# Projection start of a hybrid decoder block: fillers, first tile, first slab and first query slab cut differently

## The reference, cut to what matters

```
h = rmsnorm(x) * norm_mix
proj = h @ w_in      # q_sb,k_sb,v_sb | q_sa,k_sa,v_sa | q_idx,k_idx,w_idx | g_sb,g_sa
o_sb = stick_breaking(rmsnorm(q_sb), rmsnorm(k_sb), v_sb)
o_sa = topk_attention(rmsnorm(q_sa), rmsnorm(k_sa), v_sa, q_idx, k_idx, w_idx)
x = x + (sigmoid(g_sb) * (o_sb @ w_sb) + sigmoid(g_sa) * (o_sa @ w_sa)) @ w_out
x = x + relu(rmsnorm(x) @ w_ff1)^2 @ w_ff2
```

## Time and profile before

| | |
|---|---|
| median of 3 runs | 735.97 us (735.78 to 736.24) |
| the profiled execution | 735.93 us, of which the span is 734.2 us |
| PE busy | 727.6 us (99%) |
| DVE, ACT, POOL busy | 521.4, 336.4, 228.6 us |
| DMA moved | 70.64 MB |

### The profile page before, as it was taken

The page is one execution under the profiler, slowest core; times in us unless marked ns, Lnnn a source line. Parts: engine busy times, 40 slices in busy tenths (PEclk is TensorE's granted clock), DMA queues, the critical chain, the costliest instruction groups (busy, mean ns, idle before and its releaser), DMA issues.

```text
span 734.2 us, 9810 instructions
## 1 busy us (share of the span) xinstructions
PE 727.6 (99%) x3508; PEld 581.9 (79%) x3508; DVE 521.4 (71%) x737; ACT 336.4 (46%) x481; POOL 228.6 (31%) x194
## 2 busy tenths in 40 slices
PE   8999999999999999999999999999999999999998
PEld 5878878787777666788888988888888888888887
DVE  6355886899996755647556569695968779595972
ACT  6244753454666777723324353524335252534320
POOL 4105326000002555003301082624427080815610
PEclk9999999999999999999999999999999999999999
DMA  9308231310111212133090135142330505131102
GB/s 323 145 15 256 88 116 58 115 58 21 39 58 57 58 58 58 58 114 115 12 339 24 57 115 172 58 151 78 111 117 23 206 0 171 57 114 57 58 15 101
DMA packets 44038, 70.64 MB, mean 96 GB/s; under 512 B 2657, under 2 KB 27489, under 8 KB 44002
## 3 DMA queue, kind: packets, MB, share of 16 engines
q1 hardware_dynamic: 44000, 70.16, 29.2%
q10 hardware_dynamic: 2, 0.00, 0.0%
HBM read 65.71 MB, written 2.10 MB: 92 GB/s over the span
## 4 chain that ended last, share of the span: by engine, by line
PE 95%; DVE 1%; ACT 1%; POOL 1%; issue 1%; DMA 0%; ACTq 0%; DVEq 0%
PE ps L1754 7%; PE ps L1756 7%; PE ps L1755 7%; PE ps L419 7%; PE ps L421 7%; PE ps L420 7%; PE ps L412 7%; PE ps L414 6%; PE ps L1782 6%; PE ps L413 6%; PE ps L1784 6%; PE ps L1783 6%; PE ps L1592 2%; PE ps L1636 2%; PE ps L1668 1%; PE ps L1678 1%
## 5 line engine op out<-in xcount | busy, mean ns | idle before, releaser
L1754 PE MATMUL ps<-b_hi,cut_hi 128*128 128x512 f32 (+1 forms) x280 | 104.0, 371 | 0.0
L1755 PE MATMUL ps<-b_lo,cut_hi 128*128 128x512 f32 (+1 forms) x280 | 103.8, 371 | 0.0
L1756 PE MATMUL ps<-b_hi,cut_lo 128*128 128x512 f32 (+1 forms) x280 | 103.8, 371 | 0.0
L419 PE MATMUL ps<-cut_hi,a_hi 128*128 128x512 f32 x224 | 90.3, 403 | 0.7 <-DVE cut_lo L403 0.7
L421 PE MATMUL ps<-cut_hi,a_lo 128*128 128x512 f32 x224 | 87.6, 391 | 0.0
L420 PE MATMUL ps<-cut_lo,a_hi 128*128 128x512 f32 x224 | 87.6, 391 | 0.0
L403 DVE TENSOR_TENSOR cut_lo<-raw,cut_hi 128x2048 fp32r<-128x2048 f32 (+2 forms) x36 | 59.9, 1664 | 31.4 <-ACT cut_hi L395 31.4
L888 ACT ACTIVATE qo_sb<-ps 128x512 f32<-128x512 f32 x32 | 19.2, 600 | 135.6 <-PE ps L1756 90.9
L623 POOL TENSOR_TENSOR a_lo<-qo_sb,a_hi 128x512 fp32r<-128x512 f32 x49 | 78.2, 1619 | 5.6 <-ACT a_hi L898 5.6
L611 POOL TENSOR_SCALAR qo_sb<-qo_sb 128x128 f32<-128x128 f32 (+3 forms) x28 | 33.3, 1189 | 118.9 <-DVE snmax L1193 117.9
L395 ACT ACTIVATE cut_hi<-raw 128x2048 fp32r<-128x2048 f32 (+2 forms) x33 | 49.3, 1495 | 32.8 <-PE ps L414 22.7
(11 more groups left out here) (193 smaller groups left out, 1652.3 us busy)
## 6 DMA issues: line engine op xcount, KB each, us to landing
raw<-in_w_ff_dram SPq DMA_DIRECT2D x32, 1024.0 KB, 5.6
raw<-in_w_in_dram SPq DMA_DIRECT2D x16, 1024.0 KB, 5.6
gates<-in_x_dram SPq DMA_DIRECT2D x8, 512.0 KB, 5.9
raw<-in_w_out_dram SPq DMA_DIRECT2D x4, 1024.0 KB, 5.1
raw<-in_w_in_dram SPq DMA_DIRECT2D x4, 512.0 KB, 7.4
raw<-in_w_branch_sb_dram SPq DMA_DIRECT2D x2, 1024.0 KB, 5.0
raw<-in_w_branch_sa_dram SPq DMA_DIRECT2D x4, 512.0 KB, 6.0
out_dram<-gates SPq DMA_DIRECT2D x7, 256.0 KB, 2.0
```

The costliest lines, as they stand in the source:

```text
L419: nc.tensor.matmul(dst, l_hi, w_hi, start=start, stop=False)
L1754: T.matmul(dst, w_hi[:, w], b_hi[:, k, a:b], start=(k == 0), stop=False)
L1755: T.matmul(dst, w_hi[:, w], b_lo[:, k, a:b], start=False, stop=False)
L1756: mm = T.matmul(dst, w_lo[:, w], b_hi[:, k, a:b], start=False, stop=(k == KD - 1))
```

## The change

- The fillers' data (`cold_b`, zeros) is made first thing on DVE, without waiting for POOL, and a semaphore `cold_made` tells PE. The fillers use it as weights too. There are now six of them ahead of the gain row's spread, five behind it and seven after the first tile's transposes (before: none, four and three).
- Tile 0 is scaled in two halves of 512 columns, and each group of transposes waits for its own half.
- The first half of slab 0 is loaded, rounded and subtracted as two blocks (quarters of the slab), and the second of them is loaded behind tile 1 of x. Its rounding stands behind tile 0's first turned half on ACT.
- On DVE tile 1 is scaled ahead of the low part of tile 0's second turned half.
- Slab 2 (the first query slab) is rounded and subtracted in two halves, and PE waits for the second only at its third block.

```diff
-WARM = (4, 3)
+WARM = (6, 5, 7)
...
-            load_half(0, 0)
+            def load_quarter(k):
+                sp.dma_start(raw[:, 0, k * 512:(k + 1) * 512], rows(win, P * k, 1, GROUPS[KVI], 512).rearrange("p k c -> p (k c)")
+                             ).then_inc(half_in[k], 16)
+
+            load_quarter(0)
             sp.dma_start(x_tok[:, 1, :], x_d[P:2 * P, :]).then_inc(x_in[1], 16)
+            load_quarter(1)
             load_half(0, 1)
             load_half(1, 0)
             load_half(1, 1)
...
-                    pool.wait_ge(half_hi, 2)
-                    pool.wait_ge(half_cut, 1)
+                    pool.wait_ge(half_hi, 3)
+                    pool.wait_ge(half_cut, 2)
...
+            def act_quarter(k):
+                act.wait_ge(half_in[k], 16)
+                A(cut_slot(0, cut_hi, k, 4), raw[:, 0, k * 512:(k + 1) * 512], ACT.Copy).then_inc(half_hi, 1)
...
                 if m == 0:
-                    act_half(0)
+                    act_quarter(0)
                 elif m == 1:
                     norm_hi(0, a_hi)
+                    act_quarter(1)
                     act.wait_ge(raw_in[0], 16)
                     act_cut(0, 1, 2)
                     norm_hi(1, a_hi)
...
-                if g != KSB:
+                if g == KVI:
+                    act_half(2)
+                    act_cut(2, 1, 2)
+                elif g != KSB:
                     act_cut(2 * g + 2)
...
+            link(V.memset(cold_b[:, :], 0.0))
+            V.tensor_copy(kw_gap, cold_b[:, 0:24 * KD].rearrange("p (k c) -> p k c", k=KD)).then_inc(cold_made, 1)
             dve.wait_ge(ident_done, 1)
             dve.wait_ge(const_made, 1)
-            link(V.memset(cold_b[:, :], 0.0))
-            V.tensor_copy(kw_gap, cold_b[:, 0:24 * KD].rearrange("p (k c) -> p k c", k=KD))
...
-            norm_scale(0, x_tok[:, 0, :], x_tok[:, 0, :], mix_gain)
-            dve_half(0)
+            for hf in range(2):
+                norm_scale(0, x_tok[:, 0, hf * S:(hf + 1) * S], x_tok[:, 0, hf * S:(hf + 1) * S], bank(6 + hf))
+            dve_quarter(0)
             norm_lo(0, a_hi, a_lo)
+            dve_quarter(1)
             dve_cut(0, 1, 2)
+            norm_scale(1, x_tok[:, 1, :], x_tok[:, 1, :], mix_gain)
             norm_lo(1, a_hi, a_lo)
-            norm_scale(1, x_tok[:, 1, :], x_tok[:, 1, :], mix_gain)
             dve_cut(1, 1, 2)
...
-                if g != KSB:
+                if g == KVI:
+                    dve.wait_ge(half_hi, 4)
+                    V.tensor_tensor(cut_slot(2, cut_lo, 0, 2), raw[:, 2, 0:SLAB // 2],
+                                    cut_slot(2, cut_hi, 0, 2).bitcast(F32), ALU.subtract).then_inc(half_cut, 1)
+                    dve_cut(2, 1, 2)
...
-                pe.wait_ge(row_scaled, m + 1)
                 for hf in range(2):
                     u = 2 * m + hf
+                    pe.wait_ge(row_scaled, 1 + hf if m == 0 else m + 2)
...
-                    T.matmul(bank(3), ident_b, cold_b[:, :], start=True, stop=True)
-
+                    T.matmul(bank(3), cold_b[:, 0:P], cold_b[:, :], start=True, stop=True)
+
+            pe.wait_ge(cold_made, 1)
+            keep_warm(WARM[0])
             pe.wait_ge(one_row_made, 1)
...
-            pe.wait_ge(const_cut, 1)
-            keep_warm(WARM[0])
+            keep_warm(WARM[1])
...
-                        pe.wait_ge(half_cut, half + 1)
+                        pe.wait_ge(half_cut, 3 if half else 1)
                         pe.wait_ge(nt_cut, half + 1)
+                    if first and k == 1 and not half:
+                        pe.wait_ge(half_cut, 2)
...
+                    if (g, half, m, k) == (QSB, 0, 0, 2):
+                        slab_ready(SL_PROJ + 2 * QSB)
...
-                slab_ready(SL_PROJ + 2 * g + half)
+                if (g, half) == (QSB, 0):
+                    pe.wait_ge(half_cut, 4)
+                else:
+                    slab_ready(SL_PROJ + 2 * g + half)
...
-            keep_warm(WARM[1])
+            keep_warm(WARM[2])
```

More of the change, by code:

```diff
@@ L229, in block_kernel @@
         gains_in = sem("gains_in")
-        half_in = [sem(f"half_in{j}") for j in range(2)]
+        half_in = [sem(f"half_in{j}") for j in range(3)]
         half_hi = sem("half_hi")
@@ L264, in block_kernel @@
         kix_low = sem("kix_low")
+        cold_made = sem("cold_made")
         kix_out = sem("kix_out")
@@ L442, in load @@
                 if i == RAW + 1:
-                    sp.wait_ge(half_cut, 2)
+                    sp.wait_ge(half_cut, 3)
                 for p0, np_, nk, src in slab_source(i):
@@ L451, in load_half @@
                 sp.dma_start(dst[:, 2 * hf:2 * hf + 2, :], rows(win, 512 * i + 256 * hf, 2, GROUPS[KVI], 512)
-                             ).then_inc(raw_in[i] if hf else half_in[i], 16)
-            load_half(0, 0)
+                             ).then_inc(raw_in[i] if hf else half_in[2], 16)
+            def load_quarter(k):
+                sp.dma_start(raw[:, 0, k * 512:(k + 1) * 512], rows(win, P * k, 1, GROUPS[KVI], 512).rearrange("p k c -> p (k c)")
+                             ).then_inc(half_in[k], 16)
+            load_quarter(0)
             sp.dma_start(x_tok[:, 1, :], x_d[P:2 * P, :]).then_inc(x_in[1], 16)
+            load_quarter(1)
             load_half(0, 1)
@@ L662, in norm_hi @@
                   bank(4 + u % 2).rearrange("p (a b) -> p a b", a=4), ACT.Copy).then_inc(nt_hi, 1)
+            def act_quarter(k):
+                act.wait_ge(half_in[k], 16)
+                A(cut_slot(0, cut_hi, k, 4), raw[:, 0, k * 512:(k + 1) * 512], ACT.Copy).then_inc(half_hi, 1)
             def act_half(i):
-                act.wait_ge(half_in[i], 16)
-                A(cut_slot(i, cut_hi, 0, 2), raw[:, i, 0:SLAB // 2], ACT.Copy).then_inc(half_hi, 1)
+                if i == 1:
+                    act.wait_ge(half_in[2], 16)
+                else:
+                    act.wait_ge(*slab_arrived(i))
+                    act.wait_ge(*slab_used(i - CUT))
+                A(cut_slot(i, cut_hi, 0, 2), raw[:, i % RAW, 0:SLAB // 2], ACT.Copy).then_inc(half_hi, 1)
             act.dma_start(mix_row, norm_mix).then_inc(mix_row_in, 16)
@@ L1020, in norm_lo, with dve_quarter @@
                                 ALU.subtract).then_inc(nt_cut, 1)
[L1022 to L1025, removed]
+            def dve_quarter(k):
+                dve.wait_ge(half_hi, k + 1)
+                V.tensor_tensor(cut_slot(0, cut_lo, k, 4), raw[:, 0, k * 512:(k + 1) * 512],
+                                cut_slot(0, cut_hi, k, 4).bitcast(F32), ALU.subtract).then_inc(half_cut, 1)
             mix_gain = ps[:, 6 * S:8 * S]
             dve.wait_ge(mix_spread, 1)
-            norm_scale(0, x_tok[:, 0, :], x_tok[:, 0, :], mix_gain)
-            dve_half(0)
+            for hf in range(2):
+                norm_scale(0, x_tok[:, 0, hf * S:(hf + 1) * S], x_tok[:, 0, hf * S:(hf + 1) * S], bank(6 + hf))
+            dve_quarter(0)
             norm_lo(0, a_hi, a_lo)
+            dve_quarter(1)
             dve_cut(0, 1, 2)
+            norm_scale(1, x_tok[:, 1, :], x_tok[:, 1, :], mix_gain)
             norm_lo(1, a_hi, a_lo)
-            norm_scale(1, x_tok[:, 1, :], x_tok[:, 1, :], mix_gain)
             dve_cut(1, 1, 2)
```

## The result

The changed kernel takes 737.40 us (median of 14 runs, 735.14 to 737.90) against 735.79 us for the kernel before (14 runs, 735.64 to 736.24): ratio 1.0018, 95% interval 1.0011 to 1.0025. It is slower by 1.6 us. I had forecast 734.7 us, 1.3 us faster. Twelve of the changed kernel's runs lie between 737.17 and 737.90, two at 735.14 and 735.19; the kernel before has no such gap.

What follows compares the result with a forecast made beforehand. PE, busy 99% of the span, was taken as the bound. Span 734.2 - 0.3 (start) - 0.96 (slab 2 halves) = 732.9, plus 1.7 us around it, gave 734.7 us, range 734.1 to 736.2.

Steps and rivals of the forecast that it cites:

- I take a rise near 4.8, just behind the six fillers.: At the start, PE's clock goes from 1.2 to 2.4 GHz near 4.8 us, so the spread ends at 6.2.
- 1.9 us behind the start of full-array work: Clock timing read from the earlier trace: second run of full-array work began at 9.66, the clock rose at 11.6.
- the 7.0 of the other count: Clock rise if counted from the first full-array work (6.14 to 11.6): at 7.0 us, with 0.5 us less won.
- Rival 1: At the start, clock stays at 1.2 GHz until 11.6: 2.0 us lost, 0.96 won, 737.0 us; chance 0.12.
- Tile 1 then lands at about 7.05: Start loads: with a quarter slab less in front, tile 1 of x lands at 7.05 instead of 7.87.
- The forecast gain of 0.3 us at the start: Tile 0's second projection half: PE's second matmul at 14.62 against 14.92; gain 0.3 us, between 0 and 0.65.
- rival 3: Tile 1 lands no sooner; the quarter lengthens ACT's queue by 0.48 us: 0.3 lost, 0.96 won, 735.3; chance 0.10.
- Halves of slab 2: gain 0.96 us.: Query projection near 40 us: slab 2 in halves removes PE's wait, 0.96 us gained and passed to the end.
- Slab 0's second half lands at 9.23 again.: Start loads: the same bytes lie ahead of this half as before, so its landing stays at 9.23.
- DVE and GpSimd: Shared port at the start: DVE's subtract of slab 0 (done 11.6) must precede POOL's at 11.83, or 0.3 us goes.
- The wait for tile 3's scaling: PE's 0.4 us wait in a chain starting at its own transposes; forecast to move along with them.
- The range: Whole-kernel time meant to hold 8 in 10: 734.1 to 736.2 us, from rival 2 to above rival 4.

Runs made afterwards that it cites:

- experiment 5: Changed kernel with fourteen fillers ahead of the gain row's spread, none between spread and transposes, seven behind; 737.10 us (735.80 to 738.35), before 736.01.
- experiment 3: Changed kernel with six fillers ahead of the spread, but four and three behind it as before; 736.95 us, before 735.96.
- experiment 6: Kernel before with only the early fillers' data and six fillers ahead of the spread added, four and three behind; 737.50 us, before 736.01.
- experiment 10: Changed kernel with slab 0's first half in one piece as before, all fillers kept (six, five, seven); 737.82 us, before 735.99.
- experiment 2: Changed kernel without fillers ahead of the spread, four and three behind as before; 735.27 us, before 735.96.
- experiment 1: Kernel before with only query slab 2 rounded and subtracted in two halves; 734.71 us, before 735.96, ratio 0.9983.
- experiment 8: Changed kernel with the gain row's spread made by matmuls over all 128 array rows instead of one; 738.60 us, before 736.01.
- experiment 7: Changed kernel with two, four and three fillers and slab 0's first half in one piece as before; 735.09 us, before 736.01.
- experiment 9: Kernel before with slab 2 in halves and tile 0 scaled in two halves, fillers and loads as before; 735.29 us, before 735.99.

## Why the prediction was wrong, step by step

- **"I take a rise near 4.8, just behind the six fillers."** This step failed, and it decided the sign. The forecast had the clock rise inside the spread, so that the spread ended at 6.2. In the profile the clock rose at 13.2, and the spread ran at 1.2 GHz throughout, 3.71 us from 4.29 to 8.00. A rise that early exists (experiment 5's profile). By the run times it is the rarer case, though none of these quickest runs was profiled: 2 of 14 runs here, 2 of 11 in each of experiments 3 and 6, 3 of 12 in experiment 10. I had a single trace of before with a rise at 11.6 and read a rule into it ("1.9 us behind the start of full-array work") that the changed kernel's own trace breaks. The 4.8 does not even follow from it: 1.9 us counted from the fillers' start at 1.5 gives 3.4. It was picked between that and the 7.0 of the other count. The rule of the Trainium skill (TensorE: Matmul & The Clock Gate, "What's actually happening"), that activity releases the throttle, is not contradicted by these runs. That earlier fillers would bring the rise into the spread was my own reading of one trace.
- **Rival 1** is what happened, at 0.12. It gave 737.0 against 737.4 measured, and PE's second matmul at 16.9 against 17.82. What it missed: the spread starts at 4.22, not 4.06, and the seven fillers run nearly all at 1.2 GHz, to 13.76, while the low part that PE needs was ready at 12.45 (11.76 + 0.69). So GpSimd (17.11) was not the last to be ready; PE's own transposes, delayed by fillers, were. That 737.0 came so near to 737.40 is in part luck: rival 1 had the clock rise at 11.6 and only GpSimd on the path.
- **Landings.** "Tile 1 then lands at about 7.05" was wrong: 7.99. Landings scatter by 0.9 us between profiles (7.17 to 8.07) and a quarter slab less ahead does not show through. The forecast gain of 0.3 us at the start was not there even without the six fillers: experiment 2, with the spread where it was before, is 0.56 us slower than slab 2 alone, by the 0.5 us longer ACT queue that rival 3 describes (it put the loss at 0.3).
- **"Halves of slab 2: gain 0.96 us."** Right: 0.97 in the profile of the changed kernel, 1.0 in experiment 1's span, 1.25 in its medians. ACT and DVE kept their steps (39.35 to 41.35, 40.44 to 42.8) and no wait came behind them.
- **"Slab 0's second half lands at 9.23 again."** Not so: its load is issued at 2.84 instead of 2.23 and lands 7.2 us later, at 10.04; hidden here, because ACT comes to it at 12.15.
- **DVE and GpSimd** did not get in each other's way at the place that the prediction named: DVE's subtract of slab 0 ran from 13.22 to 14.45, GpSimd's began at 14.70.
- **The wait for tile 3's scaling** is there again, as forecast. The row names line 1019; it is the weight loads of the same transposes that wait 0.42 us for line 1012, at 23.95.
- **The range** (to 736.2) left out rival 1 and its 737.0, because I gave the clock's rise inside the spread most of the chance. Both ends follow from the prediction's own formula (1.8 and 3.55 us for the spread) and differ by more than everything else in the sum; the range should have reached to the far one.

As the sum of its parts on the medians, each the step from one kernel to the next: slab 2 -1.25, quarters and the rest of the start +0.56, six fillers ahead +1.68, one and four more behind +0.62, together the +1.61 measured. The version to keep is experiment 1: 734.71 us, against 735.96 for the kernel before on its chip. No part of the new start that was tried adds to it at the end; scaling tile 1 earlier was not tried alone.

## What to carry to other kernels

Ask of every filler what real operation stands behind it on PE, and price that operation at both clock levels: work that keeps the array busy is free only while PE waits for data anyway (two fillers here, not six). When the time of the clock's rise is taken from one trace, treat it as unknown, keep both prices in the range, and look at many runs: a gap between groups of run times can be its mark. And read a queue from its last arrival: bringing one transfer forward wins nothing if the next instruction in the queue waits for another, and splitting an instruction lengthens the queue.

## What the runs showed of the hardware that was not expected

- The clock rises at times that differ by microseconds between executions with the same work on PE: at 13.2 in the changed kernel's profile, at about 10.8 in experiment 10's, which has the same order on PE. The run times fit: changed kernel 735.14 to 737.90 us, fourteen fillers 735.80 to 738.35, where the kernel before keeps within 0.6 us in its 14 runs. Of its 104 runs beside the experiments 103 lie between 735.59 and 736.57, and one took 737.21.
- The clock can rise while PE does nothing and fall again soon (experiment 8: at 1.2 GHz in the fillers up to 4.3, 2.4 GHz at 7.3 after idling, 1.2 GHz from 8.3 to 11.6). Whether the spread's one-row matmuls have a part in the late rise stays open: experiment 8 was spoilt by its late transfer, and I ran no other.
- In thirteen of the fourteen profiles the granted clock column reads 1.00 throughout, also where PE starts at 1.2 GHz; there only the spacing of weight loads and the chain's durations show the level. In experiment 8 it does show the level (0.50 from 8.3 to 11.6), though not the 1.2 GHz of the first six fillers.
- One more DVE instruction at the start comes with 0.35 us of idle time on DVE 190 us later (experiments 7, 9, 10, but not with two or three more), which takes back what the start had won. What it waits for no profile names, so the cause stays open.
